# Hybrid encoder trunk: state-space tiles in pairs on quarters of the TensorE array, scan decay in PSUM

## The reference, cut to what matters

```python
h = rmsnorm(x)
q, k, v, u = split(h @ w_in)             # 4 x 512 columns
attn = dilated_attention(q, k, v) + relative bias      # 8 heads x 64
# state space, per direction (forward, backward) and per group of 16 channels, 64 complex states:
bu = u_g @ b_bar                          # lam_bar = exp(lam * step)
s[t] = lam_bar * s[t-1] + bu[t]
y += Re(c @ s)                            # y starts as d_skip * u
ssm = glu(gelu(y))
x = x + concat(rmsnorm(attn), rmsnorm(ssm)) @ w_out
x = x + peer(rmsnorm(x))                  # 16384 experts, 8 product-key heads, top 16
```

## Time and profile before

| | us |
|---|---|
| median of 3 runs | 2320.26 (2312.39 to 2321.18) |
| profiled execution | 2317.43 |
| its span, first to last instruction | 2315.6 |
| PE busy | 2150.3 (93%) |
| DVE busy | 1592.7 (69%) |
| ACT busy | 937.9 (41%) |
| POOL busy | 672.2 (29%) |
| granted TensorE clock, mean | 0.971 |

### The profile page before, as it was taken

The page is one execution under the profiler, slowest core; times in us unless marked ns, Lnnn a source line. Parts: engine busy times, 40 slices in busy tenths (PEclk is TensorE's granted clock), DMA queues, the critical chain, the costliest instruction groups (busy, mean ns, idle before and its releaser), DMA issues.

```text
span 2315.6 us, 38804 instructions
## 1 busy us (share of the span) xinstructions
PE 2150.3 (93%) x12654; PEld 1811.0 (78%) x12654; DVE 1592.7 (69%) x3017; ACT 937.9 (41%) x1409; POOL 672.2 (29%) x492
## 2 busy tenths in 40 slices
PE   5998899978899999999979888999789999999997
PEld 4565489977788999999855554999677889999996
DVE  5778377768777666666678872977796776666665
ACT  3333345432334444444343432554223344444443
POOL 2667157666100000000036660776660000000000
PEclk8999999989999999999989999999899999999999
DMA  4111254410457655555421112554105565555553
GB/s 179 60 59 45 109 180 165 156 64 10 139 193 253 227 186 186 190 183 189 155 79 59 59 64 106 191 180 133 45 1 191 190 227 184 188 186 185 190 183 117
DMA packets 90087, 329.10 MB, mean 142 GB/s; under 512 B 10355, under 2 KB 14579, under 8 KB 87964
## 3 DMA queue, kind: packets, MB, share of 16 engines
q1 hardware_dynamic: 89996, 328.13, 41.8%
q10 hardware_dynamic: 16, 0.02, 0.0%
HBM read 324.94 MB, written 3.16 MB: 142 GB/s over the span
## 4 chain that ended last, share of the span: by engine, by line
PE 80%; POOL 8%; issue 5%; DVE 2%; DMA 2%; POOLq 1%; ACT 1%; SPq 0%; DVEq 0%; ACTq 0%
PE ps L710 30%; PE ps L731 29%; POOL v_raw L1527 6%; PE ps L590 5%; PE ps L557 3%; PE ps L741 3%; PE ps L682 2%; POOL arena L1527 2%; PE ps L572 2%; DVE arena L1134 1%; PE ps L673 1%; PE ps L552 1%; PE ps L604 1%; PE ps L602 1%; PE ps L628 1%
## 5 line engine op out<-in xcount | busy, mean ns | idle before, releaser
L731 PE MATMUL ps<-v_hl,w_hl 128*128 128x512 f32 x3072 | 732.3, 393 | 8.2 <-DVE v_hl L1134 8.1
L731 PEld LDWEIGHTS ps<-v_hl,w_hl 128*128 128x128 f32 x3072 | 567.9, 189 | 127.9 <-DVE v_hl L1134 11.9
L710 PEld LDWEIGHTS ps<-h_hl,u_hl 128*128 128x128 f32 x4800 | 598.3, 192 | 12.7
L710 PE MATMUL ps<-h_hl,u_hl 128*128 128x256 f32 x4800 | 607.9, 283 | 0.0
L1005 ACT ACTIVATE v_hl<-v_raw 128x1024 fp32r<-128x1024 f32 x208 | 220.8, 1062 | 306.0 <-PE ps L731 281.7
L1134 DVE TENSOR_TENSOR u_hl<-u_raw,u_hl 128x1024 fp32r<-128x1024 f32 x144 | 176.5, 1225 | 197.7 <-ACT u_hl L967 197.7
L1527 POOL TENSOR_TENSOR arena<-arena 128x256 f32<-128x256 f32 (+1 forms) x240 | 263.4, 1122 | 128.5 <-DVE arena L1134 83.8
L1134 DVE TENSOR_TENSOR v_hl<-v_raw,v_hl 128x1024 fp32r<-128x1024 f32 x208 | 253.9, 1221 | 13.7 <-ACT v_hl L1005 13.4
L967 ACT ACTIVATE u_hl<-u_raw 128x1024 fp32r<-128x1024 f32 x144 | 152.9, 1061 | 247.9 <-PE ps L710 245.6
L1527 POOL TENSOR_TENSOR fence<-fence 128x1 f32<-128x1 f32 x8 | 2.0, 251 | 632.1 <-DVE arena L1318 629.8
L1134 DVE TENSOR_TENSOR arena<-arena 128x512 f32<-128x512 f32 (+4 forms) x196 | 168.5, 873 | 15.8 <-issue 6.2
(11 more groups left out here) (153 smaller groups left out, 2441.7 us busy)
## 6 DMA issues: line engine op xcount, KB each, us to landing
u_raw<-in_expert_u SPq DMA_DIRECT2D x208, 512.0 KB, 3.3
v_raw<-in_expert_v SPq DMA_DIRECT2D x208, 512.0 KB, 3.3
v_raw<-in_expert_u SPq DMA_DIRECT2D x48, 512.0 KB, 3.9
u_raw<-in_expert_v SPq DMA_DIRECT2D x48, 512.0 KB, 3.3
arena<-in_w_in SPq DMA_DIRECT2D x16, 512.0 KB, 3.7
arena<-in_w_in SPq DMA_DIRECT2D x8, 1024.0 KB, 5.4
arena<-in_ssm_b SPq DMA_DIRECT2D x16, 512.0 KB, 3.8
arena<-in_w_out SPq DMA_DIRECT2D x2, 4096.0 KB, 12.5
```

What stands on the lines that cost most here:

```text
L710: m = pe.matmul(ps[:, bank, o:o + S], hl[:, wp, k, :], h_hl[:, hp_, k, :], start=(k == 0 and j == 0), stop=(k == DC - 1 and j == 2))
L731: m = pe.matmul(ps[:, 2 * a + half, :], w_hl[s][:, wp, a * P:(a + 1) * P], v_hl[s][:, vp, half * 512:(half + 1) * 512], start=(first and j ...
```

## The change

- **Pairs on quarters of the array.** Tiles are ordered so that 0 to 3 are the forward direction and 4 to 7 the backward one. Tile n has its data in rows 32 (n % 4) of `b_sb` and `u_all`, and its B product reads only these 32 rows. Its C product writes partitions 32 (n % 4) of bank 7. `b_pair` and `c_pair` issue tiles 2p and 2p + 1 alternately and wait for both.
- **Scan decay.** `mag` is copied once per layer into PSUM bank 3, and the scan reads it there. Scores move to banks 2 and 4, the transposes follow them.
- **Rings.** `outc` and `outs` get four slots (two in `u_raw`), the C coefficients two sets. The cosine product stays on GpSimd, the sine product on VectorE.
- **Angles** are made per pair of tiles, three pairs ahead.
- **Order.** All engines go pair by pair, unrolled over the 16 pairs of a layer instead of a hardware loop over quarters. On GpSimd the first drives come ahead of the first C coefficients, and the others after the second pair of a quarter. VectorE's skip sum and attention output of a quarter come in the first pair of the next.
- **Loads.** Expert tiles 0 and 1 are loaded with 2 and 3 after the last skip sum, not at the end of the layer before.

The diff, cut to its core:

```diff
-                sp.wait_ge(s_y, 2 + (l + 1) * NT * NQ)
+                sp.wait_ge(s_y, 4 + (l + 1) * NT * NQ)
...
                 sp.wait_ge(s_ysum, 1 + NQ * (l + 1))
-                first_u(2)
-                first_u(3)
+                for k in range(4):
+                    first_u(k)
...
+                def b_pair(q, p):
+                    it, half = l * NQ + q, p // 2
...
+                    pe.wait_ge(s_pp, it * NT + 2 * p + 2)
+                    for r in range(2):
+                        for n in (2 * p, 2 * p + 1):
+                            rows = slice(32 * (n % 4), 32 * (n % 4) + 32)
+                            m = pe.matmul(ps[:, 5 + n % 2, r * S:(r + 1) * S], b_sb[rows, n, r, :],
+                                          u_all[rows, q, n // 4, :], start=True, stop=True)
...
+                def c_pair(q, p):
...
+                    pe.wait_ge(s_outc, 2 + it * NT + 2 * p + 2)
+                    pe.wait_ge(s_outs, 2 + it * NT + 2 * p + 2)
+                    for j, (kind, part) in enumerate(((0, 0), (1, 1), (2, 0), (2, 1))):
+                        for n in (2 * p, 2 * p + 1):
+                            k, o = n % 4, n // 4 * S
+                            src = (outc, outs, outs, outc)[j][n % 4]
+                            m = pe.matmul(ps[32 * k:32 * k + 32, 7, o:o + S], c_sb[q % 2][:, kind, n, :],
+                                          src[:, part, :], start=(j == 0), stop=(j == 3))
...
+                for g in range(NQ * PAIRS):
+                    q, s = divmod(g, PAIRS)
+                    if s:
+                        attention(q, s, False)
+                    if q + 1 < NQ:
+                        projections(q + 1, s, False)
+                    if g + 2 < NQ * PAIRS:
+                        b_pair((g + 2) // PAIRS, (g + 2) % PAIRS)
+                    if g:
+                        c_pair((g - 1) // PAIRS, (g - 1) % PAIRS)
+                    if q + 1 < NQ:
+                        projections(q + 1, s, True)
+                    attention(q, s, True)
+                c_pair(NQ - 1, PAIRS - 1)
...
-                    r_all = col(mag, q * NT + n).broadcast_to([P, S])
+                    r_all = ps[:, MAG_BANK, q * NT + n:q * NT + n + 1].broadcast_to([P, S])
...
+                for g in range(3):
+                    block_turns(g)
                 dve.wait_ge(s_p3, l + 1)
+                dve.tensor_copy(ps[:, MAG_BANK, 0:n_all], mag)
...
+                for g in range(NQ * PAIRS):
+                    q, s = divmod(g, PAIRS)
+                    if g + 1 < NQ * PAIRS:
+                        for j in range(2):
+                            turn_in((g + 1) // PAIRS, (g + 1) % PAIRS * 2 + j)
+                    if q and s == 0:
+                        attn_out(q - 1)
+                    scan(q, 2 * s)
+                    if s == 1:
+                        row_max(q, 0)
+                    scan(q, 2 * s + 1)
+                    if q and s == 0:
+                        y_sum(q - 1)
+                    if s == 1:
+                        row_max(q, 1)
+                    if g + 3 < NQ * PAIRS:
+                        block_turns(g + 3)
+                attn_out(NQ - 1)
+                y_sum(NQ - 1)
...
+                drives(0, 0)
+                drives(0, 1)
+                c_terms(0)
+                for g in range(NQ * PAIRS):
+                    q, s = divmod(g, PAIRS)
+                    for j in range(2):
+                        if g + 1 < NQ * PAIRS:
+                            drives((g + 1) // PAIRS, (g + 1) % PAIRS * 2 + j)
+                        turn_out(q, 2 * s + j)
+                    if s == 1 and q + 1 < NQ:
+                        c_terms(q + 1)
```

More of the change, by code:

```diff
@@ L37 @@
 NT = 8
+PAIRS = NT // 2
 PH = 8
@@ L654, in _, with attention @@
-                pe.wait_ge(s_hT, (2 * l + 1) * 4)
-                for kind in (3, 0, 1, 2):
-                    project(0, kind, 0, TT if kind == 2 else DC)
-                b_product(0, 0)
-                b_product(0, 1)
-                b_product(0, 2)
-                c_product(0, 0)
-                with pe.Fori(0, NQ - 1) as q:
-                    pe.wait_ge(s_bias, 16 * (l + 1))
-                    mix_block(q, True)
-                mix_block(NQ - 1, False)
+                def attention(q, s, late):
+                    if (s, late) == (0, True):
+                        if q == 0:
+                            pe.wait_ge(s_bias, 16 * (l + 1))
+                        scores(q, 0)
+                    if (s, late) == (1, False):
+                        scores(q, 1)
+                    if (s, late) == (2, False):
+                        prob_transposes(q, 0)
+                    if (s, late) == (2, True):
+                        values(q, 0)
+                    if (s, late) == (3, False):
+                        prob_transposes(q, 1)
+                    if (s, late) == (3, True):
+                        values(q, 1)
@@ new lines, in projections @@
+                def projections(q, s, late):
+                    for kind, lo, hi in {(0, False): ((3, 0, 4),), (0, True): ((3, 4, 8),), (1, False): ((0, 0, 3),),
+                                         (1, True): ((0, 3, 8),), (2, False): ((1, 0, 3),), (2, True): ((1, 3, 8),),
+                                         (3, False): ((2, 0, 1),), (3, True): ((2, 1, 2),)}[s, late]:
+                        project(q, kind, lo, hi)
+                pe.wait_ge(s_hT, (2 * l + 1) * 4)
+                project(0, 3, 0, DC)
@@ L912, in mix_block @@
+                copy_u(0)
+                copy_qk(0)
+                angles(0)
+                angles(1)
+                copy_v(0)
+                angles(2)
+                copy_c(0)
+                for q in range(NQ):
+                    more = q + 1 < NQ
+                    angles(q * PAIRS + 3)
+                    if q:
+                        gelu_y(q - 1)
                     if more:
                         copy_u(q + 1)
[L914 to L921 removed]
@@ L922, in mix_block @@
-                    for head in range(2):
-                        if head and more:
-                            angles(q + 1, 0)
-                        act.wait_ge(s_ptr, 1 + it * 2 + head + 1)
-                        act.activation(pT, ps[:, 4, :].rearrange("p (s a n) -> p s a n", s=2, a=TT), ACT.Copy)\
-                            .then_inc(s_pT, 1)
+                    exps(q, 0)
+                    exps(q, 1)
                     if more:
+                        angles(q * PAIRS + 4)
@@ L929, in mix_block @@
+                    copy_probs(q, 0)
+                    if more:
+                        angles(q * PAIRS + 5)
                         copy_qk(q + 1)
+                    copy_probs(q, 1)
+                    if more:
                         copy_c(q + 1)
-                    act.drain()
-                    act.wait_ge(s_ysum, 1 + it + 1)
-                    fenced(ACT.Gelu)
-                    act.activation(yT[:, bass.ds(q, 1), :].rearrange("p o n -> p (o n)"), ysum[:, 1, :],
-                                   ACT.Gelu).then_inc(s_yT, 1)
@@ L1199, in _, with block_turns @@
                 tt(angle, angle, angle_t, ALU.add)
-                def block_turns(q, half, first=False):
-                    it = l * NQ + q
-                    tiles = slice(half * NT // 2, (half + 1) * NT // 2)
-                    some = angle[:, bass.ds(q * NT + half * NT // 2, NT // 2), :]
-                    shape = [P, NT // 2, 16, 16]
+                def block_turns(g):
+                    q, p = divmod(g, PAIRS)
+                    tiles = slice(2 * p, 2 * p + 2)
+                    some = angle[:, q * NT + 2 * p:q * NT + 2 * p + 2, :]
+                    shape = [P, 2, 16, 16]
                     a_part = some[:, :, 0:16].unsqueeze(3).broadcast_to(shape)
@@ L1208, in block_turns @@
                     dve.drain()
-                    dve.wait_ge(s_outc, 1 + it * NT - (0 if half or first else NT // 2))
+                    if q:
+                        done = 2 + l * NQ * NT + 2 * (g - PAIRS + 1)
+                        dve.wait_ge(s_outc, done)
+                        dve.wait_ge(s_outs, done)
                     tt(tab[:, 0, tiles, :].rearrange("p n (a b) -> p n a b", a=16), a_part, b_part, ALU.add)
@@ L1242, in scan @@
                     dve.wait_ge(s_state, 4 + 2 * (it * NT + n + 1))
-                    tt(outs[:, s, :, :], state[:, s, :, :], two(0, n), ALU.mult).then_inc(s_outs, 1)
+                    dve.wait_ge(s_y, it * NT + n + 1)
+                    tt(outs[n % 4], state[:, s, :, :], two(0, n), ALU.mult).then_inc(s_outs, 1)
                 def row_max(q, head):
```

206 lines of the change are left out of this document (77 added, 129 removed).

## The result

The changed kernel takes 2260.8 us (median of 4 runs, 2256.4 to 2266.1), the kernel before 2319.6 (2312.4 to 2321.2): a ratio of 0.9754, interval 0.9722 to 0.9785. The profiled execution is 2258.4 us for a span of 2256.6 us, 59 less than the 2317.4 of before. The forecast was 2257.

A forecast was written before the change was run, and what follows sets the result against it. TensorE was taken to bound three of four mixer quarters, VectorE then setting the pace; 35 us saved per layer, 5 charged back, makes 60 in two layers: 2317 - 60 = 2257 us, range 2225 to 2303.

The forecast's parts named there:

- 5 charged back: Per layer, deducted from the 35 us gain for GpSimd's 0.6 us, late pair halves and a low clock after starts.
- TensorE's terms: Mixer B and C products: a pair costs one tile's time, C 1.84 us, B 1.05; 35.0 us per quarter instead of 46.6.
- TensorE is the bound in three of four quarters: Kernel before, mixer: TensorE bounds the quarters with projections, VectorE 10 us behind; VectorE leads in the last half quarter.
- my first rival: Mixer quarters: column quarters don't overlap, TensorE stays at 46.6 us; 18 us per layer, 2293 us; chance 0.12.
- The scan's price: VectorE's scans: if still contending or slower from PSUM, 0.5 us in 32 tiles, 16 us per layer.
- VectorE's pair: VectorE per pair of tiles: turn-ins 2.4, scans 2.6, sines 1.9, angles 2.6; 9.5 us in all.
- The quarter: VectorE's mixer quarter: four pairs 38.0 us plus 3.4 for row maxima, attention output and skip sum; 41.4 against 50.5.
- The start: Layer 1: angles from 31.52, three calls at 2.2 us, coefficients 3.1; first turn-in at 41.2 instead of 38.3.
- The waits for GpSimd that I charged: Mixer quarters: the C coefficients on GpSimd's queue still show as some 0.6 us per quarter.
- the fourth rival: Quarters with projections: idling TensorE's clock falls to 1.2 GHz throughout, 84 us per layer, 2425 us; chance 0.07.
- my signs of being wrong: Scans of 1.15 us, C pair 3.6, clock under 0.8 in quarters, VectorE idle for POOL or angles, ScalarE awaiting expert 0.
- Rivals 1, 2 and 3: 1: my first rival; 2: scans still contend, 2289 us, chance 0.13; 3: three-engine ring eats gain, 2317 us, chance 0.07.

## Why the prediction was right

**The total** was off by 4 us in the medians and by 1 in the profiled execution. Layer 1 gained 30.1 us up to the GLU (239.52 to 209.43) and layer 2 27 (from the addition at its start to the GLU 1125.58 to 1325.12, before 1159.73 to 1386.30): 57 of the 59 us lie where I had put them. That the sum closed so well is luck in part. GLU at 204 plus 5 charged back is 209, measured 209.43, but the 5.4 us over 204 are made up of other things than I charged for: the start came 3.7 us early, and the first quarter took 2.0 us more than I had, the two middle ones 5.1 together and the last 2.0. Behind the GLU ScalarE takes expert 0 at 226.82, 17.4 us after the GLU starts, exactly as in the earlier trace rows. So the expert loads stay hidden, as said.

**TensorE's terms** were right: from start to start a C pair takes 1.85 us (I had 1.84) and a B pair 1.06 (1.05), and a quarter with the clock at 0.96 has 35.72 us of work (35.0). The one guess, that column quarters overlap as fully as row ones, holds for tiles issued in alternation. The small price for changing shape stayed in both, which is what the Trainium skill's rule on draining between tiling modes (TensorEngine Tiling (Array Packing), section Key Properties) would give; it decided nothing.

**"TensorE is the bound in three of four quarters" failed** as an explanation, though not as a description of the chain. Had it been so, giving back the overlap should have cost the 18 us per layer of my first rival; it cost 9 to 13 in the whole kernel. And an edit of VectorE's operand alone, in the kernel before, should have brought almost nothing; it brought 20. The rival's price was too high on both sides: it had quarters of 48.0 us against 42.6, and they were 46.5 and 45.8 against 43.9 and 44.0. Six kernels make the case:

| order and rings | decay in | overlap on TensorE | median, us | GLU of layer 1, us |
|---|---|---|---|---|
| old | SBUF | none | 2314 | 239.52 |
| old | PSUM | none | 2294 | 228.65 |
| new | SBUF | B, and C in part | 2312 | 238.47 |
| new | SBUF | both | 2307 | 235.97 |
| new | PSUM | none | 2271 | 217.73 |
| new | PSUM | both | 2262 | 209.91 |

The decay alone brings 20 us, all the rest without it 7, together they bring 52. Each bound hid the other: with the decay in SBUF VectorE keeps the quarter at 50 us and more, and with the decay alone in PSUM it stays at 48. The new order, which brings next to nothing with the decay in SBUF, brings 23 us with it in PSUM (2294 to 2271, no overlap in either), and the overlap 9 more. So by far the largest part, 43 of 52 us, is the decay and the order together, and the overlap that my forecast put first is the smallest. Which part of the new order does it (pairs, rings, angles, the place of the coefficients, the loads) no run separates, and none has the overlap in the old order.

**The scan's price was too low.** I had 0.5 us in 32 tiles, 16 per layer. The experiment gives 22 per layer in the new order: beside the scans themselves the sines and angle operations around them got slower too, by 11 us in layer 1. That the PSUM operand escapes was right to 0.69 us at most. The Trainium skill, SBUF — State Buffer, section Who interferes with whom, has this rule: a second SBUF input is what meets GpSimd's reads. The runs agree on the scan: 654 to 691 ns with one SBUF input, 657 to 1749 with two.

**VectorE's pair** came out at 9.88 instead of 9.5 by two errors against each other. Sines: 0.61 from start to start instead of 0.96, since each starts just ahead of a GpSimd product (120.89 against 120.94, and 122.80 against 122.82), and then it is GpSimd that waits: its cosine product at 122.82 takes 1.80 us, the one at 192.16, beside turn-ins, 1.27. The same section has this as well: the order of issue decides who is blocked. Angles with their drain: 3.7 instead of 2.6, since each operation starts in the middle of a GpSimd product. I had added contention where the old order had it, and should have laid GpSimd's work beside VectorE's in the new order. That the pair is only 0.4 us off is luck.

**The quarter** was 43.9 us instead of 41.4 plus 1.2 charged back. Four pairs explain 1.5 of the difference to 41.4; the other 1.0 is covered by a wait that I didn't have, the skip sum for C with 1.50 to 1.74 us. I looked at ScalarE's angles only for their own result and not for what stands behind them in its queue. Moving one call took the wait away, and 2.5 us per layer from the middle quarters.

**The start** was 37.49 us, not 41.2. Of this 3.1 us are the parameters (19.33 instead of 22.45), with the first expert loads off the queue in front of them, and 0.6 the three angle calls at 2.0 instead of 2.2: the loads too are a part that I costed at nothing while it brought a little. The waits for GpSimd that I charged (0.6 us a quarter) did not show in the middle; in the last quarter they did, on both engines. First VectorE's timeline, then PE's:

```profile
198.95 1.27 DVE L1275 TENSOR_TENSOR_SCAN arena<-ps,arena 128x256 f32<-128x256 f32 x2 [1.22 <-POOL arena L1565]
```

```profile
201.50 3.40 PE L594 MATMUL ps<-arena,c_more 128*32 128x256 f32 x16 [3.00 <-POOL arena L1565]
...
205.87 1.92 PE L594 MATMUL ps<-u_raw,c_more 128*32 128x256 f32 x16
209.43 1.12 PE L692 MATMUL ps<-arena 128*128 128x512 f32 x2 [1.65 <-ACT arena L947]
```

It took 38.3 us where I had 36.3: without angles GpSimd is as slow as VectorE, as the text said, and a C pair at a low clock takes 3.4.

**The clock** fell, as the fourth rival feared, but to 0.89, 0.96, 0.88 and 0.78 by quarter and not to the half level throughout. TensorE has over a quarter of its time free in the last one, so part of it is hidden; how much is not, no run tells. Of my signs of being wrong this one came true (under 0.8, in the last quarter), and so did a VectorE that waits for GpSimd, once; neither undid the gain. Rivals 1, 2 and 3 did not happen.

## What to carry to other kernels

Where two engines are close to each other, here TensorE at 47 and VectorE at 40 of 51 us, the chain of waits can name one bound and hide the other: test with an edit that touches only the second. A broadcast operand that costs nothing to copy into PSUM can free a VectorE operation from GpSimd; here that was worth 20 us in the old order and 45 in the new one. When the order of an engine changes, take each duration beside what will then run on the other engine, and read every call that stands behind a moved one in its queue.

## What was unexpected of the hardware

- Products on different row quarters ran side by side even when they were issued tile by tile (eight records in 1.14 us); those on different column quarters did so fully only in alternation (sixteen in 1.92 us, 2.81 tile by tile). In both, records of the second tile started before the first tile's last ones, so they don't start in the order of issue: the second B tile 0.01 us behind the first, the second C tile 0.89 us behind. Row and column quarters aren't the only difference, since a B tile has four records here and a C tile eight; no run separates the two.
- The rounding of the angles, an operation with one SBUF input, is slowed beside GpSimd as well: 0.43 us clean at 31.07, 0.79 in the plain pairs, 1.33 at 105.28; into PSUM it was 0.43 every time, for half the columns. I had expected this of operations with two SBUF inputs only. The Trainium skill, SBUF — State Buffer, section Who interferes with whom, has this exception: a tensor_scalar can run in a mode that takes both ports and then contends. That 512 columns from SBUF to SBUF take no longer than 256 into PSUM fits such a mode.
- With less work for TensorE its granted clock was lower: 1.00 in both middle quarters of the kernel without overlap, where it was busy 45.91 of 46.54 us and 45.16 of 45.79, but 0.96 and 0.88 in those of the changed kernel (35.72 of 43.89 and 38.95 of 44.00), and 0.78 at 27.74 of 38.34, where a C pair took 3.63 us at 175.47. The busy share alone doesn't give it: the last half quarter before the change had 1.00 at 22.79 of 30.50. The falls lengthen TensorE's own work; how much of that reaches the total, no run shows.
